# Low weight halves made in block 0, kept in DRAM, and loaded by the later blocks, in a float32 hybrid encoder layer on one core

## Chip, cores and metric

One Trainium2 chip, one core of it. The metric is device microseconds of one execution of the whole kernel, lower is better. Kernel before: median 4028.33 us of three runs (4001.9 to 4049.22).

## What is computed

One layer of a streaming encoder, on 2048 prompt frames and 32 sample frames, width 1024, all in float32 (`FF` is 2816):

```python
h = rmsnorm(x, g_pre_mix)
q, k, v, u, g = split_projection(h, w_in)          # u = u_a * sigmoid(u_b)
attn = prompt_attention(q, k, v, table, sink)      # 16 heads, window 128 + own chunk of 64
y = depthwise_conv(u_hist, w_dw) + b_dw            # width 31, 1024 channels
conv = silu(layernorm(y, ln_g, ln_b)) @ w_conv_out
m = g[:, :, 0] * attn + g[:, :, 1] * conv
x = x + rmsnorm(m @ w_out, g_post_mix)
h = rmsnorm(x, g_pre_ffn)
f = (silu(h @ w_ffn_gate) * (h @ w_ffn_up)) @ w_ffn_down
x = x + rmsnorm(f, g_post_ffn)
```

TensorE takes its fast four-byte type (fp32r), which keeps fewer bits than float32. So each operand `a` is split into `a_hi` (rounded to fp32r) and `a_lo = a - a_hi`, and each product is three: `hi*hi + hi*lo + lo*hi`.

## The kernel before

**Blocks and steps.** The tokens go in `NB` = 4 blocks of `T` = 512 columns; block 3 takes the 32 sample tokens too (544 columns, two groups of 272). Each block walks the same `NS` = 124 steps. One step is one 128x1024 float32 piece of weights (512 KB). The kinds, in order: 16 `glu_b`/`glu_a` (alternating), 8 `q`, 1 `k`, 1 `v`, 16 `gate`, 8 `conv`, 8 `out`, 44 `ffn_gate`/`ffn_up` (alternating), 22 `down`. The names `S_Q, S_K, S_A, S_C, S_W, S_F, S_D` are the first steps of q, k, gate, conv, out, ffn and down. `G(b, s) = b * NS + s` counts steps over the whole kernel; all 124 pieces are read anew in every block.

**Weights.** A piece passes three engines before TensorE (PE) may use it. SP loads it into one of `RAW` = 3 raw buffers (`load_weights`, L371), for the step three ahead, once `w_lo` of the piece that held the buffer is made. ScalarE (ACT) rounds it to `w_hi` (`split_hi`, L785); it waits for the raw piece and for `w_used`, that is for PE to have finished the step two before, since `w_hi` and `w_lo` have two buffers each. GpSimd (POOL) makes `w_lo = w_raw - w_hi` (`split_lo`, L465). PE waits for `w_lo` (`weights`), then does the step's matmuls, 24 of 512 columns as a rule (`feature_major`, L570; `token_major`, L606 to L608). ACT and POOL split the piece of step s+1 at the head of their work for step s.

**Beside the steps.** Every engine's order is written out by hand.
- VectorE (DVE) does the depthwise convolution, 248 tap instructions (`conv`, L1041 and L1045) a block, spread over steps 4 to 41 by `conv_ops`: 7 a step in glu, q, k, v, and 6 a step in the gate steps. Each is a SCALAR_TENSOR_TENSOR of two SBUF tensors, `y += u * dw`.
- Each of the 16 gate steps also carries one attention unit (4 heads x 128 queries): PE scores (L642 to L644), DVE `score_max` (L1108, writes `p`), ACT exponentials (`exps`, L875), DVE `denominator` (L1125, L1126), POOL `p * rl` (L510), PE transposes of `p` (L654), ACT `pt_hi` (L869), DVE `pt_lo` (L1120), PE product with the values (L671 to L673). `p` is one buffer: `score_max` of the next unit waits for the transposes of this one. PE's order in a gate step: scores(n), transposes(n-1), the step's 24 weight matmuls, values(n-1). DVE's order: `score_max(n)`, `pt_lo(n-1)`, 2 taps, `denominator(n)`, on odd n `qs_lo`, 4 taps.
- Step `S_C` waits for the LayerNorm of the convolution. After the last `out` step ACT, POOL and DVE do the norm after the mix and the one before the FFN, tile by tile (POOL L474, L476; DVE `scale_rows`, L1056), with the split of step `S_F + 1` between them; `first_ffn_steps` starts on the first tiles.
- At the end of a block the FFN's norm and residual run beside the first two steps of the next block (step 1 of block 3 waits for them on PE). In step 1 SP waits for that residual, and then stores the 2 MB block of `y_prompt` (`store_y`, L382).
- Further DMAs on SP's queue: `g_post` at `S_C`, 2 MB of x at `S_W`, 512 KB x tiles of the next block in `down`.

SP's loop body before, in the order of its issues, starts so:

```python
for b in range(NB):
    for s in range(NS):
        load_weights(G(b, s) + RAW)
        if s == 1 and b:
            store_y(b - 1)
```

## Time and profile before

| | |
|---|---|
| runs | 4028.33 us median, 4001.9 to 4049.22 |
| span of the profiled execution | 4055.0 us |
| PE matmul busy | 3463.3 us, 85% of the span |
| DVE / POOL / ACT busy | 2033.5 / 1602.4 / 1242.6 us (50 / 40 / 31%) |
| `w_lo` on POOL | 1337.3 us, 496 instructions |
| `w_hi` on ACT | 524.9 us, 496 instructions |
| DMA | 74 GB/s over the span, 289.22 MB read from HBM, 12.17 MB written |
| mean granted TensorE clock | 0.916 of full speed |

How to read it: busy is the time in which at least one instruction of the engine ran; matmuls are pipelined and their ends are modelled, so PE busy counts a little more than the work. A group's row reads: line, engine, operation, output <- inputs, shapes, count | busy us, mean ns of one | idle time of the engine just before, and what ended it. PEclk is the granted clock of TensorE as a share of full speed. Times in timelines are from the start of the span. The times of the runs are of other executions than the profiled one.

### The profile page before, as it was taken

Reading aid. Unit: us, or ns where it says so; the run is one execution under the profiler, and the core shown is the slowest. Engines: PE = TensorE matmul, PEld = TensorE weight load, DVE = VectorE, ACT = ScalarE, POOL = GpSimd, SP = SyncE. Lnnn points to the kernel's source line nnn. Section 1 sums busy time; section 2 is a strip of 40 time slices with the busy share of each in tenths; the row PEclk is TensorE's granted clock in tenths of the full one; section 3 lists DMA queues with packets and bytes.
Section 4 is the critical chain, followed back from the end, with each engine's and each line's share of the span. In section 5 each row is a group of like instructions: output and inputs, shape, how many; then the busy total and the mean of one; then the engine's idle time right before and its main releaser. Section 6 shows DMA issues by size and latency. Waiting matters only on the chain.

```text
span 4055.0 us, 42574 instructions
## 1 busy us (share of the span) xinstructions
PE 3463.3 (85%) x17022; PEld 2870.9 (71%) x17022; DVE 2033.5 (50%) x2660; ACT 1242.6 (31%) x1986; POOL 1602.4 (40%) x778
## 2 busy tenths in 40 slices
PE   2378877999997878999979878999978878969997
PEld 2256656887776656887757656887878866869986
DVE  1296963004599962005696962005495963230033
ACT  1013452224323442224213452224212433122222
POOL 1154433444444433444453433444454422233432
PEclk8689988999999988999989988999988976679999
DMA  1212112223321112233311112223211110212221
GB/s 58 82 63 68 47 47 84 99 95 108 114 83 47 47 64 82 94 98 106 113 60 55 47 58 85 96 94 110 100 58 59 48 32 31 71 47 89 86 81 60
DMA packets 88165, 300.92 MB, mean 74 GB/s; under 512 B 10338, under 2 KB 17586, under 8 KB 87330
## 3 DMA queue, kind: packets, MB, share of 16 engines
q1 hardware_dynamic: 87968, 298.21, 22.0%
q8 instruction: 135, 2.21, 0.2%
q14 instruction: 62, 0.50, 0.0%
HBM read 289.22 MB, written 12.17 MB: 74 GB/s over the span
## 4 chain that ended last, share of the span: by engine, by line
PE 56%; DVE 18%; issue 13%; POOL 9%; ACT 3%; DMA 1%; SPq 0%; POOLq 0%; DVEq 0%; ACTq 0%
PE PS L570 35%; DVE y L1045 12%; POOL w_lo L465 6%; PE PS L606 5%; PE PS L608 5%; PE PS L607 5%; POOL p L510 3%; PE PS L684 1%; PE PS L690 1%; DVE PS L1086 1%; PE PS L587 1%; DVE p L1108 1%; DVE x L1091 1%; DVE xs L1056 1%; DVE pt_lo L1120 1%
## 5 line engine op out<-in xcount | busy, mean ns | idle before, releaser
L465 POOL TENSOR_TENSOR w_lo<-w_raw,w_hi 128x1024 fp32r<-128x1024 f32 x496 | 1337.3, 2697 | 1791.8 <-ACT w_hi L785 1790.7
L570 PE MATMUL PS<-h_hi,w_hi 128*128 128x512 f32 (+1 forms) x3352 | 1088.9, 358 | 241.8 <-POOL w_lo L465 185.6
L785 ACT ACTIVATE w_hi<-w_raw 128x1024 fp32r<-128x1024 f32 x496 | 524.9, 1058 | 2077.9 <-PE PS L570 1502.0
L570 PE MATMUL PS<-h_hi,w_lo 128*128 128x512 f32 (+1 forms) x3352 | 1084.1, 357 | 0.0
L570 PE MATMUL PS<-h_lo,w_hi 128*128 128x512 f32 (+1 forms) x3352 | 1075.2, 354 | 0.0
L1045 DVE SCALAR_TENSOR_TENSOR y<-u,dw,y 128x512 f32<-128x512 f32 (+1 forms) x960 | 1011.5, 1118 | 0.0
L570 PEld LDWEIGHTS PS<-h_hi,w_hi 128*128 128x128 f32 x3352 | 601.2, 192 | 334.0 <-POOL w_lo L465 184.2
L570 PEld LDWEIGHTS PS<-h_lo,w_hi 128*128 128x128 f32 x3352 | 601.2, 192 | 90.2
L570 PEld LDWEIGHTS PS<-h_hi,w_lo 128*128 128x128 f32 x3352 | 599.0, 192 | 84.3
L1290 DVE TENSOR_TENSOR f<-PS,tmp 128x512 f32<-128x512 f32 (+1 forms) x88 | 61.6, 700 | 892.6 <-PE PS L570 868.6
L510 POOL TENSOR_TENSOR p<-p,small 128x1024 f32<-128x1024 f32 x68 | 157.2, 2312 | 464.8 <-DVE small L1126 464.8
L1296 DVE TENSOR_TENSOR f_lo<-f,f_hi 128x1024 fp32r<-128x1024 f32 (+1 forms) x88 | 208.9, 2374 | 249.5 <-ACT f_hi L999 249.5
L606 PE MATMUL PS<-w_hi,f_hi 128*128 128x512 f32 x748 | 296.7, 397 | 12.2 <-DVE f_lo L1296 8.4
L608 PE MATMUL PS<-w_hi,f_lo 128*128 128x512 f32 x748 | 295.1, 394 | 0.0
L607 PE MATMUL PS<-w_lo,f_hi 128*128 128x512 f32 x748 | 294.2, 393 | 0.0
L875 ACT ACTIVATE p<-p,small 128x256 f32<-128x256 f32 x272 | 135.1, 498 | 280.5 <-DVE small L1115 280.5
L606 PEld LDWEIGHTS PS<-w_hi,f_hi 128*128 128x128 f32 x748 | 140.5, 188 | 48.1 <-DVE f_lo L1296 10.8
L570 PE MATMUL PS<-act_hi,w_hi 128*128 128x512 f32 x320 | 131.8, 452 | 46.4 <-DVE act_lo L1260 46.4
L608 PEld LDWEIGHTS PS<-w_hi,f_lo 128*128 128x128 f32 x748 | 140.5, 188 | 33.0
L607 PEld LDWEIGHTS PS<-w_lo,f_hi 128*128 128x128 f32 x748 | 140.5, 188 | 32.5
L552 PE MATMUL PS<-ident_sb,xs 128*128 128x128 f32 x272 | 54.5, 368 | 108.5 <-DVE xs L1056 108.5
L1108 DVE CUSTOM_DVE_ANT_0 p<-PS,bias,sink_sb 128x256 f32<-128x256 f32 x272 | 114.9, 475 | 37.5 <-PE PS L654 27.8
(166 smaller groups left out, 3800.3 us busy)
## 6 DMA issues: line engine op xcount, KB each, us to landing
w_raw<-in_w_stream SPq DMA_DIRECT2D x496, 512.0 KB, 3.3
xs<-in_x_prompt SPq DMA_DIRECT2D x16, 512.0 KB, 3.7
x<-in_x_prompt SPq DMA_DIRECT2D x4, 2048.0 KB, 8.5
out_y_prompt<-x SPq DMA_DIRECT2D x4, 2048.0 KB, 7.3
gp<-in_g_post SPq DMA_DIRECT2D x4, 1024.0 KB, 4.8
toep_dram<-toep_dram SPq DMA_DIRECT2D x1, 3048.0 KB
bias<-toep_dram SPq DMA_DIRECT2D x1, 2048.0 KB, 8.6
bias<-toep_dram SPq DMA_DIRECT2D x2, 1024.0 KB, 5.8
```

Source lines behind the costliest of these rows:

```text
L465: nc.gpsimd.tensor_tensor(w_lo[:, g % 2, :], w_raw[:, g % RAW, :], w_hi[:, g % 2, :].bitcast(F32), ALU.subtract).then_inc(w_lo_ok, 1)
L510: nc.gpsimd.tensor_tensor(p[:], p[:], rl.unsqueeze(2).broadcast_to([P, 4, 2 * P]), ALU.mult).then_inc(p_ok, 1)
L570: last = nc.tensor.matmul(PS[:, k0 + off, 0:n], w, x[:, k, c0:c0 + n], start=first and k == 0, stop=stop and k == KT - 1)
L606: nc.tensor.matmul(out, hi, wk[0], start=first, stop=False)
L607: nc.tensor.matmul(out, hi, wk[1], start=False, stop=False)
L608: last = nc.tensor.matmul(out, lo, wk[0], start=False, stop=last_k)
L785: A(w_hi[:, g % 2, :], w_raw[:, g % RAW, :], ACT.Copy).then_inc(w_hi_ok, 1)
L875: A(p[:, h, :], p[:, h, :], ACT.Exp, bias=nmx[:, h:h + 1], accum_out=lsum[:, h:h + 1])
L1045: ins = STT(out, src, dw[:, ct, k:k + 1], out, ALU.mult, ALU.add)
L1108: nc.vector.tensor_tensor_reduce(out=p[:, h, :], in0=PS[:, 2 + h // 2, (h % 2) * 2 * P:(h % 2 + 1) * 2 * P], in1=bias[:, head, :], scale=1 ...
L1290: TT(over(b, f[:, j, 0:c]), z(b, r), over(b, tmp[:, j % 2, 0:c]), ALU.mult).then_inc(z_dve, 1)
L1296: TT(f_lo[:, dd % 2, :, 0:c], f[:, 2 * kp:2 * kp + 2, 0:c], f_hi[:, dd % 2, :, 0:c].bitcast(F32), ALU.subtract).then_inc(flo_ok, 1)
```

## The change

In block 0 nothing changes in how weights are split, but SP also stores each `w_lo` piece to a DRAM tensor (`keep_lo`). In blocks 1 to 3 SP loads two 512 KB pieces a step into the three raw buffers, the raw piece and its low half from DRAM (`load_halves`), for the step two ahead; ACT copies both with rounding, one into `w_hi` and one into `w_lo`; POOL makes no `w_lo`; PE waits for the count `w_got` of ACT's copies. A raw buffer is free again when ACT has copied the half that stood in it. `j = half(g, lo)` numbers the loads: one a step in block 0, two a step after.

```diff
+        w_lo_dram = nc.dram_tensor("w_lo_dram", [NS, P, D], F32, kind="Internal").ap()
...
+        def half(g, lo):
+
+            return g if g < NS else NS + 2 * (g - NS) + lo
...
-            def load_weights(g):
+            def load_half(j, src):
+
+                if j >= NS + RAW:
+                    sp.wait_ge(w_got, j - RAW - NS + 1)
+                elif j >= RAW:
+                    sp.wait_ge(w_lo_ok, j - RAW + 1)
+                sp.dma_start(w_raw[:, j % RAW, :], src).then_inc(raw_in[j % RAW], 16)
+
+            def load_halves(g):
                 if g >= NB * NS:
                     return
-                if g >= RAW:
-                    sp.wait_ge(w_lo_ok, g - RAW + 1)
-                sp.dma_start(w_raw[:, g % RAW, :], w_stream[g % NS]).then_inc(raw_in[g % RAW], 16)
+                s = g % NS
+                load_half(half(g, 0), w_stream[s])
+                sp.wait_ge(lo_out[s % 2], 16 * (s // 2 + 1))
+                load_half(half(g, 1), w_lo_dram[s])
+
+            def keep_lo(g):
+
+                sp.wait_ge(w_lo_ok, g + 1)
+                sp.dma_start(w_lo_dram[g], lo_of(g).bitcast(F32)).then_inc(lo_out[g % 2], 16)
...
             for b in range(NB):
                 for s in range(NS):
-                    load_weights(G(b, s) + RAW)
+                    if b == 0:
+                        keep_lo(s)
+                        if s + RAW < NS:
+                            load_half(s + RAW, w_stream[s + RAW])
+                    if G(b, s) + 2 >= NS:
+                        load_halves(G(b, s) + 2)
                     if s == 1 and b:
                         store_y(b - 1)
...
             def split_lo(g):
-                if g is None:
+                if g is None or g >= NS:
                     return
                 pool.wait_ge(w_hi_ok, g + 1)
                 if g >= 2:
                     pool.wait_ge(w_used, g - 1)
+                    pool.wait_ge(lo_out[g % 2], 16 * (g // 2))
...
             def weights(g):
-                pe.wait_ge(w_lo_ok, g + 1)
+                if g < NS:
+                    pe.wait_ge(w_lo_ok, g + 1)
+                else:
+                    pe.wait_ge(w_got, 2 * (g - NS) + 2)
...
-                act.wait_ge(raw_in[g % RAW], 16 * (g // RAW + 1))
+                j = half(g, 0)
+                act.wait_ge(raw_in[j % RAW], 16 * (j // RAW + 1))
                 if g >= 2:
                     act.wait_ge(w_used, g - 1)
-                A(w_hi[:, g % 2, :], w_raw[:, g % RAW, :], ACT.Copy).then_inc(w_hi_ok, 1)
+                if g < NS:
+                    A(hi_of(g), w_raw[:, j % RAW, :], ACT.Copy).then_inc(w_hi_ok, 1)
+                    return
+                A(hi_of(g), w_raw[:, j % RAW, :], ACT.Copy).then_inc(w_got, 1)
+                j = half(g, 1)
+                act.wait_ge(raw_in[j % RAW], 16 * (j // RAW + 1))
+                act.wait_ge(lo_out[g % 2], 16 * (NS // 2))
+                A(lo_of(g), w_raw[:, j % RAW, :], ACT.Copy).then_inc(w_got, 1)
```

`hi_of(g)` and `lo_of(g)` are the buffers `w_hi[:, g % 2, :]` and `w_lo[:, g % 2, :]` as before; PE's matmuls and their order are the same.

**POOL, the gate steps of block 1.** Before, `w_lo` pieces and the attention units' products `p * rl` take turns (x16 each; three of them shown):

```order
111 L510 TENSOR_TENSOR p<-p,small 128x1024 [waits rl_ok]
112 L465 TENSOR_TENSOR w_lo<-w_raw,w_hi 128x1024 [waits w_used,w_hi_ok]
113 L510 TENSOR_TENSOR p<-p,small 128x1024 [waits rl_ok]
114 L465 TENSOR_TENSOR w_lo<-w_raw,w_hi 128x1024 [waits w_used,w_hi_ok]
115 L510 TENSOR_TENSOR p<-p,small 128x1024 [waits rl_ok]
```

After, on POOL at the same place, with what stands just before (the norm of block 0's end) and behind (the gates of `S_C`):

```order
203 L520 TENSOR_TENSOR prs<-prs,neghalf 128x1 [waits pool_chain]
204 L542 TENSOR_TENSOR p<-p,small 128x1024 [waits rl_ok] x16
205 L549 TENSOR_TENSOR gates<-gates,q 128x512 [waits o_out,sig_ok]
```

From block 1 on the only large products on POOL are those of attention and of the gates; between the end of block 0 and the gate steps of block 1 it has none.

**ACT, two gate steps of block 1.** Before (`gates` is the copy of a gate result out of PSUM, `q` the copy of an attention result, `p` the exponentials):

```order
448 L875 ACTIVATE p,small<-p,small 128x256 [waits mx_ok]
449 L875 ACTIVATE p,small<-p,small 128x256 x3
450 L876 ACTIVATE small<-small 128x4
451 L852 ACTIVATE qs_hi<-q 128x512 [waits z_act,qk_done]
452 L785 ACTIVATE w_hi<-w_raw 128x1024 [waits w_used,raw_in1]
453 L925 ACTIVATE gates<-PS 128x512 [waits w_used]
454 L869 ACTIVATE pt_hi<-PS 128x1024 [waits pv_done,pt_done]
```

and after:

```order
481 L918 ACTIVATE p,small<-p,small 128x256 [waits mx_ok]
482 L918 ACTIVATE p,small<-p,small 128x256 x3
483 L919 ACTIVATE small<-small 128x4
484 L895 ACTIVATE qs_hi<-q 128x512 [waits z_act,qk_done]
485 L824 ACTIVATE w_hi<-w_raw 128x1024 [waits w_used,raw_in1]
486 L828 ACTIVATE w_lo<-w_raw 128x1024 [waits lo_out1,raw_in2]
487 L968 ACTIVATE gates<-PS 128x512 [waits w_used]
488 L912 ACTIVATE pt_hi<-PS 128x1024 [waits pv_done,pt_done]
```

One more ACTIVATE of 128x1024, which waits for a second load, stands ahead of `gates` and `pt_hi`.

**SP, where block 1 begins.** Before, the store of y stands among single loads:

```order
33 L371 DMA w_raw<-in_w_stream 128x1024 [waits w_lo_ok] x18
34 L382 DMA out_y_prompt<-x_60 128x4x1024 [waits pn_ok]
35 L371 DMA w_raw<-in_w_stream 128x1024 [waits w_lo_ok] x41
```

After, it stands between pairs; row 277 is the low half of step 3 of block 1, rows 279 and 280 are the pair of step 4:

```order
271 L397 DMA w_lo_dram<-w_lo 128x1024 [waits w_lo_ok]
272 L384 DMA w_raw<-in_w_stream 128x1024 [waits w_lo_ok]
273 L384 DMA w_raw<-w_lo_dram 128x1024 [waits w_got,lo_out1]
274 L384 DMA w_raw<-in_w_stream 128x1024 [waits w_got]
275 L384 DMA w_raw<-w_lo_dram 128x1024 [waits w_got,lo_out0]
276 L384 DMA w_raw<-in_w_stream 128x1024 [waits w_got]
277 L384 DMA w_raw<-w_lo_dram 128x1024 [waits w_got,lo_out1]
278 L408 DMA out_y_prompt<-x_60 128x4x1024 [waits pn_ok]
279 L384 DMA w_raw<-in_w_stream 128x1024 [waits w_got]
280 L384 DMA w_raw<-w_lo_dram 128x1024 [waits w_got,lo_out0]
```

Before, the load issued just ahead of the store was that of step 4; after, it is that of step 3.

## Rows read from the trace of the kernel before

**Rows 1.** The page: the span, and the chain that ended last, by line.
```profile
span 4055.0 us, 42574 instructions
...
PE PS L570 35%; DVE y L1045 12%; POOL w_lo L465 6%; PE PS L606 5%; PE PS L608 5%; PE PS L607 5%; POOL p L510 3%; PE PS L684 1%; PE PS L690 1%; DVE PS L1086 1%; PE PS L587 1%; DVE p L1108 1%; DVE x L1091 1%; DVE xs L1056 1%; DVE pt_lo L1120 1%
```
**Rows 2.** Stretches: us; PE, PEld, DVE, ACT, POOL busy; PEclk, DMA share, GB/s.
```profile
1071.00:1174.00 103.00, 93.46 (x386) 74.63 (x385) 91.20 (x103) 25.04 (x34) 47.55 (x28) 0.95 0.29 100
1174.00:1236.00 62.00, 60.18 (x311) 50.68 (x309) 62.00 (x63) 15.07 (x20) 27.09 (x10) 1.00 0.28 91
1236.00:1427.00 191.00, 156.72 (x780) 123.75 (x780) 185.13 (x320) 80.29 (x201) 82.93 (x31) 0.96 0.14 45
...
1966.00:2067.00 101.00, 91.78 (x386) 73.40 (x385) 89.59 (x101) 25.06 (x34) 50.02 (x28) 0.97 0.30 107
2067.00:2159.00 92.00, 66.78 (x308) 55.00 (x307) 61.63 (x80) 14.55 (x19) 48.13 (x10) 0.83 0.18 57
2159.00:2340.00 181.00, 156.87 (x784) 124.08 (x783) 172.09 (x304) 80.39 (x199) 79.38 (x31) 0.98 0.14 47
...
2882.00:3000.00 118.00, 101.59 (x769) 100.57 (x768) 93.19 (x115) 25.00 (x33) 51.92 (x28) 0.93 0.27 93
3000.00:3102.00 102.00, 74.33 (x551) 73.72 (x550) 67.11 (x83) 15.20 (x19) 51.37 (x10) 0.85 0.15 52
3102.00:3290.00 188.00, 165.46 (x1167) 151.25 (x1166) 178.31 (x309) 81.52 (x202) 79.28 (x31) 0.97 0.14 44
...
1620.00:1780.00 160.00, 160.00 (x697) 130.68 (x696) 9.71 (x15) 38.04 (x44) 69.83 (x29) 1.00 0.29 96
```
**Rows 3.** The two splits, each line by itself: count, ns min/median/max.
```profile
L465 POOL TENSOR_TENSOR w_lo<-w_raw,w_hi x496: 2339/2411/21333, 43.0 to 4019.4; 128x1024 fp32r<-128x1024 f32 x166
...
L785 ACT ACTIVATE w_hi<-w_raw x496: 1038/1061/1067, 41.8 to 4018.3; 128x1024 fp32r<-128x1024 f32 x166
```
**Rows 4.** Timeline of DVE over one gate step of block 1: start, us.
```profile
1275.09 0.47 DVE L1108 CUSTOM_DVE_ANT_0 p<-PS,bias,sink_sb 128x256 f32<-128x256 f32 x1
...
1277.10 1.22 DVE L1120 TENSOR_TENSOR pt_lo<-PS,pt_hi 128x1024 fp32r<-128x1024 f32 x1
...
1279.84 6.48 DVE L1045 SCALAR_TENSOR_TENSOR y<-u,dw,y 128x512 f32<-128x512 f32 x4
1286.25 0.47 DVE L1108 CUSTOM_DVE_ANT_0 p<-PS,bias,sink_sb 128x256 f32<-128x256 f32 x1
```
**Rows 5.** Timeline of POOL over the same gate step.
```profile
1280.00 2.31 POOL L510 TENSOR_TENSOR p<-p,small 128x1024 f32<-128x1024 f32 x1 [6.71 <-DVE small L1126]
1282.28 2.83 POOL L465 TENSOR_TENSOR w_lo<-w_raw,w_hi 128x1024 fp32r<-128x1024 f32 x1
```
**Rows 6.** Timelines of POOL and of DVE in the q steps of block 2.
```profile
2085.79 22.23 POOL L465 TENSOR_TENSOR w_lo<-w_raw,w_hi 128x1024 fp32r<-128x1024 f32 x2 [10.14 <-ACT w_hi L785]
...
2083.35 19.96 DVE L1045 SCALAR_TENSOR_TENSOR y<-u,dw,y 128x512 f32<-128x512 f32 x30
```
**Rows 7.** Timeline of ACT in the FFN steps of block 1.
```profile
1642.04 1.06 ACT L785 ACTIVATE w_hi<-w_raw 128x1024 fp32r<-128x1024 f32 x1 [4.46 <-PE PS L570]
...
1647.56 1.06 ACT L785 ACTIVATE w_hi<-w_raw 128x1024 fp32r<-128x1024 f32 x1 [3.98 <-PE PS L570]
```
**Rows 8.** DMA issues: count, KB each, median us from issue to landing.
```profile
w_raw<-in_w_stream SPq DMA_DIRECT2D x496, 512.0 KB, 3.3
...
x<-in_x_prompt SPq DMA_DIRECT2D x4, 2048.0 KB, 8.5
```
**Rows 9.** The beginning of block 1: timelines of SP and of ACT.
```profile
1086.19 0.39 SPq L382 DMA_DIRECT2D out_y_prompt<-x  x1
...
1096.22 1.06 ACT L785 ACTIVATE w_hi<-w_raw 128x1024 fp32r<-128x1024 f32 x1 [6.22 <-DMA w_raw<-in_w_stream]
```
**Rows 10.** Timeline of DVE in the norms before the FFN, block 1: two tiles' scaling.
```profile
1579.42 2.82 DVE L1056 TENSOR_SCALAR xs<-x,rstd 128x1024 f32<-128x1024 f32 x1 [0.72 <-POOL rstd L476]
...
1586.52 0.75 DVE L1056 TENSOR_SCALAR xs<-x,rstd 128x1024 f32<-128x1024 f32 x1 [0.73 <-POOL rstd L476]
```

More of the change, by code:

```diff
@@ L171, in build @@
         w_hi_ok, w_lo_ok = sem("w_hi_ok"), sem("w_lo_ok")
-        w_used = sem("w_used")
+        w_used, w_got = sem("w_used"), sem("w_got")
+        lo_out = [sem("lo_out0"), sem("lo_out1")]
         z_act, z_dve = sem("z_act"), sem("z_dve")
@@ L233, in result_out, with hi_of, lo_of @@
                 eng.wait_ge(z_dve, by_dve(b, s))
+        def hi_of(g):
+            return w_hi[:, g % 2, :]
+        def lo_of(g):
+            return w_lo[:, g % 2, :]
+        def half(g, lo):
+            return g if g < NS else NS + 2 * (g - NS) + lo
         def norm_tile(b, tt, second):
@@ L393, in _ @@
             for g in range(RAW):
-                load_weights(g)
+                load_half(g, w_stream[g])
             for tt in range(1, 4):
@@ L565, in feature_major @@
                         pe.wait_ge(alo_ok, b * KT + k + 1)
-                    hi, lo = (w[:, g % 2, k * P:(k + 1) * P] for w in (w_hi, w_lo))
-                    for w, x, first, stop in ((hi, x_hi, True, False), (hi, x_lo, False, False),
-                                              (lo, x_hi, False, True)):
+                    hi, lo = (t[:, k * P:(k + 1) * P] for t in (hi_of(g), lo_of(g)))
+                    for wt, x, first, stop in ((hi, x_hi, True, False), (hi, x_lo, False, False),
+                                               (lo, x_hi, False, True)):
                         for c0, n, off in parts:
-                            last = nc.tensor.matmul(PS[:, k0 + off, 0:n], w, x[:, k, c0:c0 + n],
+                            last = nc.tensor.matmul(PS[:, k0 + off, 0:n], wt, x[:, k, c0:c0 + n],
                                                     start=first and k == 0, stop=stop and k == KT - 1)
@@ L583, in first_ffn_steps @@
                         for k in range(KT):
-                            hi, lo = (w[:, g % 2, k * P:(k + 1) * P] for w in (w_hi, w_lo))
-                            for w, x, first, stop in ((hi, h_hi, True, False), (hi, h_lo, False, False),
-                                                      (lo, h_hi, False, True)):
-                                last = nc.tensor.matmul(out, w, x[:, k, c0:c0 + n],
+                            hi, lo = (t[:, k * P:(k + 1) * P] for t in (hi_of(g), lo_of(g)))
+                            for wt, x, first, stop in ((hi, h_hi, True, False), (hi, h_lo, False, False),
+                                                       (lo, h_hi, False, True)):
+                                last = nc.tensor.matmul(out, wt, x[:, k, c0:c0 + n],
                                                         start=first and k == 0, stop=stop and k == KT - 1)
@@ L600, in token_major @@
                         hi, lo = x_hi[:, kts[kk], t0:t0 + P], x_lo[:, kts[kk], t0:t0 + P]
-                        wk = [w[:, g % 2, kk * T:(kk + 1) * T] for w in (w_hi, w_lo)]
+                        wk = [t[:, kk * T:(kk + 1) * T] for t in (hi_of(g), lo_of(g))]
                         first, last_k = i == 0 and kk == 0, i == n_half - 1 and kk == 1
@@ L619, in values_of @@
                         hi, lo = h_hi[:, k, t0:t0 + P], h_lo[:, k, t0:t0 + P]
-                        wk = [w[:, g % 2, k * P:(k + 1) * P] for w in (w_hi, w_lo)]
+                        wk = [t[:, k * P:(k + 1) * P] for t in (hi_of(g), lo_of(g))]
                         nc.tensor.matmul(out, hi, wk[0], start=k == 0, stop=False)
```

## The prediction, made before the changed kernel was run

> **What bounds the kernel now.** I read the page first: its span and the chain that ended last. Then the busy times by stretch, since the kernel goes through stages with different limits, and last the timelines at the places where PE is not busy. The chain [rows 1] runs mostly over PE's weight matmuls, but DVE's taps have 12% of it, `w_lo` on POOL 6% and `p * rl` 3%. So something beside PE holds it for a fifth of the time, and the reader is to find where.
>
> The stretches [rows 2] answer that. They are, for blocks 1, 2 and 3, the glu steps, the q, k, v steps and the gate steps, and as the last row a piece of the FFN. In the FFN PE is busy for 160.00 of 160 us at full granted clock; `w_hi` copies follow each other there every 1647.56 - 1642.04 = 5.52 us [rows 7], which is PE's own pace for a step of 512 columns. Nothing can be won there. In glu PE has 9.5, 9.2 and 16.4 us without work, in q, k, v 1.8, 25.2 and 27.7 us, in the gate steps 34.3, 24.1 and 22.5 us. In two q, k, v stretches the granted clock is also down, at 0.83 and 0.85.
>
> The timelines show why. On DVE one gate step lasts from `score_max` at 1275.09 to the next at 1286.25, 11.16 us, and the four taps at its end take 6.48 us [rows 4]. Thirty taps with nothing beside them that gets through take 19.96 us, 0.665 each [rows 6], so four should take 2.7. The missing 3.8 us lie exactly beside the two POOL products [rows 5]: `p * rl` (2.31) and `w_lo` (2.83). DVE and POOL do not run side by side here; each stops the other. In the q steps it is turned round: two `w_lo` need 22.23 us while DVE runs its thirty taps, and one reaches 21.3 us against a median of 2.4 [rows 3, 6]. PE then waits for `w_lo`.
> By the Trainium skill, page "SBUF — State Buffer", section "SBUF: two separate sides", a DVE operation with two SBUF inputs and a POOL operation exclude each other for the whole instruction, and whichever starts first has the port. The first half agrees with these rows; by the second half POOL would wait for one tap of 0.7 us and not for thirty, so there the trace decides.
>
> **The change part by part.**
>
> *POOL loses 372 of 496 `w_lo`.*
> (a) q, k, v. No `w_lo` can starve there. Block 1 shows the stage nearly without a stall, 62 us. Block 2 goes from 92 to 61, block 3 from 102 to 62 x 544/512 + 2 = 68, block 1 loses 1: 31 + 34 + 1 = 66 us.
> (b) Gate steps. DVE's step loses the part of the 3.8 us that `w_lo` causes. The first tap behind `p * rl` waits about 2.31 - 0.66 = 1.65; the rest, 2.2, is `w_lo`'s. 11.16 - 2.2 = 9.0, and steps with an odd unit have `qs_lo` more (128x512 like a tap, about 0.6): 9.3 on average. PE is busy for 156.72 / 16 = 9.8 us a step, an overcount, at a clock of 0.96; at full clock about 9.4. Both engines then have nearly the same load, so I take 9.6, with the first step longer: 155 us for the stage, 163 in block 3. That is 191 - 155, 181 - 155 and 188 - 163: 36 + 26 + 25 = 87 us. Bounds: if PE's busy time stays as it is (157, 157, 165), 81; if all of DVE's 16 x 2.2 came through in each block, 105. The bound from the other side is rival B.
> (c) glu. Fourteen taps (9.3 us) and one `u` (128x512 too, 0.7) now fit into two PE steps (11.04), where two `w_lo` with 2.2 each made 14.4. PE's floor is 16 x 5.52 = 88 us (94 to 97 in block 3). See (e) for what is given back.
> (d) Norms before the FFN. `w_lo` of step `S_F + 1` holds the scaling of tile 2 for 2.82 us instead of 0.75 [rows 10], on the way to PE's transposes; ACT's second copy puts 1.06 on the same chain ahead of it. Net 1.0 us a block, and about as much for the same in `down`: 6 us in all. Bounds: 0 to 12.
>
> *SP's queue.* (e) A pair is loaded for the step two ahead, not three. In step 1 SP waits for the residual and then puts the 2 MB of y into the queue. Before, the load behind it was that of step 5, and ACT got it at 1096.22, 10.0 us after the store [rows 9]. Now it is the pair of step 4. With the residual a microsecond earlier (POOL starts its norm without a `w_lo` in front) the first half arrives at about 1095.5, the second 1.3 to 1.7 later, and ACT is done near 1098; PE, which began the block at 1071, wants it at 1071 + 4 x 5.52 = 1093. That is 5 us lost in blocks 1 and 2; in block 3 PE itself waits for that residual in step 1 and the loads land meanwhile (12 us of wait remain). So glu goes 103 to 93, 101 to 93, 118 to 97 + 12 = 109: 27 us. Bounds: 17 to 36. Behind the store only SP's own later loads are queued, and ACT waits for those in order, so a late half also holds ACT's sigmoid; PE needs that only two steps later.
>
> *ACT gets 372 more copies* at 1.06 us [rows 3]. Steady state: `w_used` fires, both copies take 2.1 us, where copy and `w_lo` took 1.06 + 2.41 = 3.5 us before; PE needs the pair 5.52 us after. In a gate step ACT has 80.29 / 16 = 5.0 us of work [rows 2] and would have 6.1 of 9.6. The copies start when PE ends the weight matmuls; `pt_hi` stands behind them and `gates`: 3.2 us later, with an attention copy (two at 1.06, two of half the size); PE's values, scores and transposes, the rest of its step (9.4 - 5.5 = 3.9), come before `pt_hi` can start. Cover of half a microsecond, priced at nothing; if it fails, `pt_lo` and DVE's whole step come later (rival B).
>
> *DMA.* Two loads of 512 KB a step: 190 GB/s in the FFN, where one is 96 GB/s at a DMA share of 0.29 [rows 2], so 0.58. A load takes 3.3 us from issue to landing, 2 MB take 8.5 [rows 8]: 1.7 us more for each further 512 KB, 3.4 us a pair if loads overlap, against 5.52. The low half of step g+2 is issued when ACT has copied the high half of g+1 (1.1 us into PE's step g) and must be in ACT's hands some 8.7 us later; it takes 3.3 to 5. Hidden.
> By the Trainium skill, page "DMA: Bandwidth & Descriptors", section "Anatomy of one DMA — SWDGE (gpsimd) path", a DMA costs 2.0 us fixed and its bytes at 436 GB/s, 3.2 us here, and its "Rules for kernel authors" ask for 1 MiB or more per DMA; that speaks against many small loads. One load agrees with it. Two one after the other would be 6.4 us by the page, more than PE's step; that is rival A.
>
> *Block 0* stores 124 low halves. SP waits for `w_lo` there anyway before a load; the store goes ahead of that load. Three raw buffers cover it, except at the start where PE waits for the first late load: +2 us (0 to 10).
>
> **Sum.** -66 - 87 - 27 - 6 + 2 = -184 us. Against the profiled execution, 4055 - 184 = 3871. Its span is 27 us over the median of the runs; if that is only how the execution was taken, the median becomes 4028 - 184 = 3844. The stalls in q, k, v differ from block to block in one execution (2, 25, 28 us), so part of the 27 is likely one stall more, which the change removes in any case, and the true number lies nearer 3871 by that part. I take 3855.
>
> **The rivals.**
>
> *A, the other side: pairs do not overlap and a pair takes 2 x 3.3 = 6.6 us.* Three half buffers leave little ahead. Then 82 steps (conv, out, FFN, down) of blocks 1 and 2 take 1.08 us longer each, +177; the FFN of block 3 +24; glu +8 in place of -27; q, k, v -43 in place of -66; the gate steps keep -87: 79 us slower, 4107. It decides from about 6.3 us for a pair. Against it: the 8.5 us for 2 MB, which are four loads' bytes, and the low DMA share. 5%.
>
> *B, a new wait in the gate steps.* ACT's second copy makes `pt_hi` late, or the loop from transposes over scores, exponentials and `p * rl` holds at some 10.7 us. The gain there is half, 44: 3900. For it: half a microsecond of cover. Against it: ACT is busy 40% there. 13%.
>
> *C, nothing to be seen.* The stalls move: DVE, no longer stopped, is stopped by PE, and the starts of the blocks lose more (15 us each, twice) while the gate stage stays. Then only (a) less 30 is left: 3992 to 4020. 4%.
>
> *D, my forecast,* 3810 to 3890: 78%.
>
> **How the numbers follow.** One per cent, 40 us, is about what a measurement can tell from no change. D, B and most of C are beyond it on the fast side, A on the slow side: faster 0.92, same 0.03, slower 0.05. The range goes from 3805 (gate at its better bound, glu too, the lower base) to 3915 (rival B with the upper base), which leaves out A, C and little of D.
>
> **What the profile will show.** Right, if DVE taps in blocks 1 to 3 are long only beside `p * rl`; q, k, v are near 61 us and gate steps near 9.6; FFN steps stay at 5.52 us with the DMA share near 0.6; one PE stall of 5 us stands at step 4 of blocks 1 and 2. Wrong, if ACT's copies wait for DMA in FFN steps (A), or if gate steps stay over 10.5 us with PE waiting for `pt_lo` or `p` (B).

## The result, and the profile after

The changed kernel takes 3835.91 us (median of 4 runs, 3831.98 to 3857.77), the kernel before, run beside it, 4037.47 us (4 runs, 4001.9 to 4049.22): ratio 0.9505, 95% interval 0.9456 to 0.9555. The forecast was 3855, with 3805 to 3915 as its range. The profiled execution of after took 3835.48 us, with a span of 3833.6; the span of before's was 4055.0 [rows 1].

The page of after: span, busy times, and the chain that ended last.

```profile
span 3833.6 us, 43442 instructions
...
PE 3409.4 (89%) x17022; PEld 2850.4 (74%) x17022; DVE 1698.6 (44%) x2660; ACT 1596.7 (42%) x2358; POOL 586.3 (15%) x406
...
PE 74%; DVE 4%; ACT 3%; issue 1%; POOL 1%; DMA 0%; SPq 0%; DVEq 0%; ACTq 0%; POOLq 0%
```

DVE's taps had 12% of the chain and `w_lo` 6% [rows 1]; now all of DVE has 4% and all of POOL 1%. DVE is busy for 335 us less (1698.6 against 2033.5) with the same 2660 instructions: that is the time for which POOL had made its instructions longer. The line numbers of after are: `w_hi` L824 (L822 in block 0), `w_lo` by ACT L828, `w_lo` by POOL L497, taps L1088, weight matmuls L605. Groups of after: count, busy us and mean ns.

```profile
L824 ACT ACTIVATE w_hi<-w_raw 128x1024 fp32r<-128x1024 f32 x372 | 394.6, 1061 | 1177.9 <-PE PS L605 876.3
L1088 DVE SCALAR_TENSOR_TENSOR y<-u,dw,y 128x512 f32<-128x512 f32 (+1 forms) x960 | 837.9, 939 | 0.0
...
L497 POOL TENSOR_TENSOR w_lo<-w_raw,w_hi 128x1024 fp32r<-128x1024 f32 x124 | 322.1, 2598 | 487.3 <-ACT w_hi L822 369.6
L828 ACT ACTIVATE w_lo<-w_raw 128x1024 fp32r<-128x1024 f32 x372 | 387.6, 1042 | 4.0 <-DMA w_raw<-w_lo_dram 4.0
```

The second copy costs ACT 1.04 us, and in the whole kernel it waited 4.0 us for its DMA. Where the time went shows by stages, each measured from the last weight matmul of the stage ahead to its own last one (us; in a cell the time before, then after):

| | glu | q, k, v | gate | conv | out | FFN | down | block |
|---|---|---|---|---|---|---|---|---|
| block 0 | 254 / 260 | 93 / 61 | 184 / 192 | 92 / 90 | 46 / 46 | 273 / 273 | 130 / 130 | 1071 / 1051 |
| block 1 | 103 / 95 | 62 / 60 | 191 / 157 | 90 / 85 | 46 / 46 | 273 / 270 | 131 / 127 | 895 / 839 |
| block 2 | 101 / 95 | 93 / 60 | 181 / 157 | 91 / 85 | 46 / 46 | 273 / 270 | 132 / 128 | 916 / 840 |
| block 3 | 118 / 107 | 102 / 67 | 188 / 166 | 218 / 214 | 59 / 59 | 310 / 310 | 155 / 156 | 1150 / 1080 |

In blocks 1 to 3: glu -25, q, k, v -69, gate -80, conv -14, FFN -6, down -7, and block 0 -19: together 221, the difference of the spans. Stretches of after, to be laid beside [rows 2]: us; PE, PEld, DVE, ACT, POOL busy; PEclk, DMA share, GB/s.

```profile
1051.00:1147.00 96.00, 90.85 (x389) 73.79 (x388) 70.80 (x109) 40.47 (x50) 4.82 (x12) 0.98 0.57 198
1147.00:1207.00 60.00, 59.95 (x311) 50.77 (x309) 46.98 (x72) 24.13 (x29) 0.00 (x0) 1.00 0.50 176
1207.00:1364.00 157.00, 152.82 (x783) 125.92 (x784) 145.09 (x310) 98.91 (x223) 36.05 (x16) 0.97 0.32 108
...
1985.00:2046.00 61.00, 60.72 (x314) 51.42 (x312) 47.35 (x72) 24.64 (x30) 0.00 (x0) 1.00 0.51 176
...
2838.00:2906.00 68.00, 67.72 (x555) 67.58 (x554) 52.02 (x74) 24.85 (x30) 0.00 (x0) 1.00 0.46 157
...
1620.00:1780.00 160.00, 159.22 (x696) 129.80 (x695) 14.65 (x19) 69.34 (x77) 0.80 (x2) 1.00 0.56 196
```

In q, k, v PE has at most 0.3 us of idle time left; in block 1 it has 5 us in glu and 4 us in the gate stage, where it had 9.5 and 34.3. The FFN piece has a DMA share of 0.56, and PE is as busy as before; the 0.8 us without PE are the start of `down` at 1764.

### The profile page after: what moved, and what is told of

Read it like the earlier page. It is cut to its first block, busy times and chain, and to the rows that moved or that the text cites. A ratio compares the mean times of both kernels' runs of the same rounds, so it can differ in the third digit from the quotient of the medians.

```text
span 3833.6 us, 43442 instructions
## 1 busy us (share of the span) xinstructions
PE 3409.4 (89%) x17022; PEld 2850.4 (74%) x17022; DVE 1698.6 (44%) x2660; ACT 1596.7 (42%) x2358; POOL 586.3 (15%) x406
## 4 chain that ended last, share of the span: by engine, by line
PE 74%; DVE 4%; ACT 3%; issue 1%; POOL 1%; DMA 0%; SPq 0%; DVEq 0%; ACTq 0%; POOLq 0%
PE PS L605 47%; PE PS L641 6%; PE PS L643 6%; PE PS L642 6%; PE PS L689 1%; PE PS L677 1%; PE PS L622 1%; DVE PS L1129 1%; DVE x L1134 1%; PE PS L678 1%; PE PS L679 1%; PE PS L706 1%; PE PS L725 1%; PE PS L707 1%; PE PS L708 1%
## 5 line engine op out<-in xcount | busy, mean ns | idle before, releaser
L605 PE MATMUL PS<-h_hi,w_hi 128*128 128x512 f32 (+1 forms) x3352 | 1077.7, 355 | 147.5 <-POOL w_lo L497 118.9
L605 PE MATMUL PS<-h_hi,w_lo 128*128 128x512 f32 (+1 forms) x3352 | 1077.6, 355 | 0.0
L605 PE MATMUL PS<-h_lo,w_hi 128*128 128x512 f32 (+1 forms) x3352 | 1068.7, 352 | 0.0
L824 ACT ACTIVATE w_hi<-w_raw 128x1024 fp32r<-128x1024 f32 x372 | 394.6, 1061 | 1177.9 <-PE PS L605 876.3
L1088 DVE SCALAR_TENSOR_TENSOR y<-u,dw,y 128x512 f32<-128x512 f32 (+1 forms) x960 | 837.9, 939 | 0.0
L605 PEld LDWEIGHTS PS<-h_hi,w_hi 128*128 128x128 f32 x3352 | 594.7, 190 | 232.0 <-POOL w_lo L497 112.6
L605 PEld LDWEIGHTS PS<-h_lo,w_hi 128*128 128x128 f32 x3352 | 595.0, 190 | 89.9
L605 PEld LDWEIGHTS PS<-h_hi,w_lo 128*128 128x128 f32 x3352 | 593.8, 190 | 83.4
L497 POOL TENSOR_TENSOR w_lo<-w_raw,w_hi 128x1024 fp32r<-128x1024 f32 x124 | 322.1, 2598 | 487.3 <-ACT w_hi L822 369.6
L828 ACT ACTIVATE w_lo<-w_raw 128x1024 fp32r<-128x1024 f32 x372 | 387.6, 1042 | 4.0 <-DMA w_raw<-w_lo_dram 4.0
L822 ACT ACTIVATE w_hi<-w_raw 128x1024 fp32r<-128x1024 f32 x124 | 131.2, 1059 | 536.5 <-PE PS L605 331.1
L1339 DVE TENSOR_TENSOR f_lo<-f,f_hi 128x1024 fp32r<-128x1024 f32 (+1 forms) x88 | 134.1, 1524 | 331.5 <-ACT f_hi L1042 330.7
L605 PE MATMUL PS<-act_hi,w_hi 128*128 128x512 f32 x320 | 131.9, 452 | 46.3 <-DVE act_lo L1303 46.3
```

Source lines behind the costliest of these rows:

```text
L497: nc.gpsimd.tensor_tensor(w_lo[:, g % 2, :], w_raw[:, g % RAW, :], w_hi[:, g % 2, :].bitcast(F32), ALU.subtract).then_inc(w_lo_ok, 1)
L605: last = nc.tensor.matmul(PS[:, k0 + off, 0:n], wt, x[:, k, c0:c0 + n], start=first and k == 0, stop=stop and k == KT - 1)
L822: A(hi_of(g), w_raw[:, j % RAW, :], ACT.Copy).then_inc(w_hi_ok, 1)
L824: A(hi_of(g), w_raw[:, j % RAW, :], ACT.Copy).then_inc(w_got, 1)
L828: A(lo_of(g), w_raw[:, j % RAW, :], ACT.Copy).then_inc(w_got, 1)
L1088: ins = STT(out, src, dw[:, ct, k:k + 1], out, ALU.mult, ALU.add)
```

## Profile after: two places where PE still waits

The first gate step of a block. Timelines of ACT, DVE and PE in block 1 of after: start, us, what ended the idle time before.

```profile
1207.04 1.06 ACT L824 ACTIVATE w_hi<-w_raw 128x1024 fp32r<-128x1024 f32 x1 [8.18 <-PE PS L658]
1208.00 1.04 ACT L828 ACTIVATE w_lo<-w_raw 128x1024 fp32r<-128x1024 f32 x1
1208.95 0.58 ACT L966 ACTIVATE v_hi<-PS 128x512 fp32r<-128x512 f32 x1
1209.43 0.62 ACT L895 ACTIVATE qs_hi<-q 128x512 fp32r<-128x512 f32 x1
```
```profile
1210.24 0.68 DVE L1140 TENSOR_TENSOR qs_lo<-q,qs_hi 128x512 fp32r<-128x512 f32 x1
```
```profile
1211.18 0.55 PE L677 MATMUL PS<-k_hi,qs_hi 64*128 64x256 f32 x1 [4.23 <-DVE qs_lo L1140]
```

And that step as a stretch (columns as above):

```profile
1207.00:1222.00 15.00, 10.82 (x38) 8.82 (x39) 8.16 (x19) 6.57 (x15) 2.31 (x1) 0.66 0.20 71
```

PE waits for 4.23 us for `qs_lo`, which stands behind four ACT copies; the granted clock of the step is 0.66, a mixture of the 2.4 and the 1.2 GHz level. This step takes 14.8 us.

The fifth glu step of blocks 1 and 2 (step 4). SP, ACT and PE in block 1 of after:

```profile
1066.07 0.39 SPq L408 DMA_DIRECT2D out_y_prompt<-x  x1
```
```profile
1075.70 1.06 ACT L824 ACTIVATE w_hi<-w_raw 128x1024 fp32r<-128x1024 f32 x1 [11.12 <-DMA w_raw<-in_w_stream]
1076.98 1.06 ACT L828 ACTIVATE w_lo<-w_raw 128x1024 fp32r<-128x1024 f32 x1 [0.22 <-DMA w_raw<-w_lo_dram]
1077.94 0.58 ACT L954 ACTIVATE tmp<-PS 128x512 f32<-128x512 f32 x1
```
```profile
1078.66 0.76 PE L605 MATMUL PS<-h_hi,w_hi 128*128 128x512 f32 x1 [5.15 <-ACT tmp L954]
```

ACT has the raw half 9.6 us after the 2 MB store was issued and the low half 1.3 us later, and PE stands still for 5.15 us. The last half microsecond is the sigmoid `tmp` of step 2, which ACT does behind the two copies and which PE needs for step 4. The prediction had seen the sigmoid held up, and had taken it for needed only later.

## The experiments

Eleven kernels, in four groups; each group had runs of before beside it, and each ratio is against those. Stage and step times are of the one profiled execution of each kernel.

**Stores alone.** The changed kernel with every `w_lo` of block 0 stored and none loaded back: the two functions that say so are these, and POOL makes all 496 `w_lo` as before.

```diff
+        def kept(s):
+            return s < NS
+
+        def dram(g):
+            return False
```

> The kernel before, with one part of the change: block 0 also stores its 124 low halves in DRAM; nobody reads them, and POOL makes all 496 w_lo as before. Theory L (DVE and POOL exclude each other; w_lo on POOL in blocks 1 to 3 was the whole cost): the time of before, ratio 0.995 to 1.005, block 0 at about 1071 us give or take the stalls in its q steps. Rival S (the stores in block 0 shift or shorten block 0, which was 19 us shorter in the changed kernel's trace): ratio about 0.995, block 0 near 1051 us, its q, k, v steps near 61 us.

4041.75 us (10 runs), ratio 1.002 [0.9981, 1.0058]; block 0 takes 1072 us in its profile, 1071 before. The interval of the ratio, 16 us to either side, shows no cost of the stores, but the trace does: the first four steps of block 0 take 180.8 us in place of 175.9 (179.8 in the changed kernel). There POOL's third `w_lo` waits for the store of the first, which stands in SP's queue behind the DMAs of the start. The stores are not the cause of block 0's -19 us either.

**POOL rounds the loaded low half.** Loads as in the changed kernel, but for blocks 1 to 3 POOL makes `w_lo` out of the loaded low half and zeros, the same instruction as before with two inputs:

```diff
-                A(lo_of(g), w_raw[:, j % RAW, :], ACT.Copy).then_inc(w_got, 1)
+                    nc.gpsimd.tensor_tensor(halves[0], halves[1], zero[:].unsqueeze(1).broadcast_to([P, KT, P]),
+                                            ALU.subtract).then_inc(w_lo_ok, 1)
```

> The changed kernel, but POOL rounds the low half that came from DRAM into w_lo (a TENSOR_TENSOR of 128x1024 that subtracts a tile of zeros), where ACT copies it in the changed kernel. All loads are those of the changed kernel. Theory L: most of the gain is gone, since POOL again holds what DVE's taps need: ratio to before 0.985 to 1.01, gate steps at 11 to 12 us, stalls of 5 to 20 us in q steps. Rival P (the gain came from the low halves being ready in DRAM, from the shorter way from the raw piece to PE): ratio 0.95 to 0.96, gate steps at 9.6 us, because POOL's instruction no longer waits for ACT's.

4041.73 us (10 runs, 4019 to 4080), ratio 1.0039 [0.9992, 1.0086]: the whole gain is gone, with the DMAs of the changed kernel in place. Its gate stages are 191, 181 and 187 us, within 0.5 us of those of before. Timelines of POOL and DVE in one gate step of it:

```profile
1402.17 2.31 POOL L554 TENSOR_TENSOR p<-p,small 128x1024 f32<-128x1024 f32 x1 [6.71 <-DVE small L1172]
1404.44 2.84 POOL L501 TENSOR_TENSOR w_lo<-w_raw,zero 128x1024 fp32r<-128x1024 f32 x1
```
```profile
1402.01 6.48 DVE L1091 SCALAR_TENSOR_TENSOR y<-u,dw,y 128x512 f32<-128x512 f32 x4
```

They are the rows of before over again (2.31, 2.83 and 6.48 [rows 4, 5]). So the gain comes from POOL doing less, and not from the low halves being ready in DRAM.

**POOL copies the low half.** The same, with a copy that has one input:

```diff
+                    nc.gpsimd.tensor_copy(lo_of(g), w_raw[:, j % RAW, :]).then_inc(w_lo_ok, 1)
```

> As the kernel in which POOL rounds the low half, but with a TENSOR_COPY of 128x1024, which has one SBUF input. Theory L1 (any long POOL instruction that reads SBUF stops DVE's taps, whatever the number of its inputs): about the time of before, 0.99 to 1.01, gate steps 11 to 12 us. Rival L2 (only a POOL instruction with two SBUF inputs stops them): DVE's taps stay at 0.74 us beside it and the time is that of the changed kernel, about 0.95. In between, 0.96 to 0.98, if the copy is just shorter than the subtraction (2.4 us).

3914.84 us (3898 twice, 3931 and 3932), ratio 0.9691 [0.9637, 0.9745]: between the two. One gate step on POOL and DVE:

```profile
1250.65 2.31 POOL L552 TENSOR_TENSOR p<-p,small 128x1024 f32<-128x1024 f32 x1 [6.72 <-DVE small L1170]
1252.91 1.50 POOL L500 CAST w_lo<-w_raw 128x1024 fp32r<-128x1024 f32 x1
```
```profile
1250.49 5.13 DVE L1089 SCALAR_TENSOR_TENSOR y<-u,dw,y 128x512 f32<-128x512 f32 x4
```
```profile
L500 POOL CAST w_lo<-w_raw x372: 1036/1044/24450, 1047.0 to 3859.6; 128x1024 fp32r<-128x1024 f32 x186
```

With both products on POOL four taps take 6.48 us, with product and copy 5.13, with the product alone 4.37 (below). The last row (ns min, median, max) shows that the copy takes 1.04 us as a rule; beside the taps it took 1.50, and one lasted 24.45 us. A short operation starves as a long one does, and each q, k, v stage is 11 to 27 us longer than in the changed kernel. By the Trainium skill, page "SBUF — State Buffer", section "Who interferes with whom", a DVE instruction with two SBUF inputs contends with a GpSimd instruction that reads SBUF. The copy reads it, if with one input only, and the 5.13 us agree.

**Low halves from DRAM in some stages only.** Two kernels in which pairs are loaded for a part of the steps; the others are loaded and split as in block 0. `kept(s)` decides both what is stored and what is loaded:

```diff
+        def kept(s):
+            return s < S_C
```

> Low halves are kept and loaded for the 42 steps of glu, q, k, v and gate alone; for conv, out, FFN and down of every block POOL makes w_lo as before. Theory L: nearly the whole gain, since DVE has its taps only there; lost are the norms before the FFN and the transposes in down, 3 + 4 us in blocks 1 and 2 each: ratio 0.953 to 0.957, about 3850 us. Rival F (the 66 FFN and down steps with a pair of loads each were slowed by the loads, or sped by the missing w_lo): more than 15 us away from the changed kernel on either side.

3855.27 us (3853.3 to 3857.8), ratio 0.9555 [0.9501, 0.9608]. Blocks 1 and 2 take 850 and 852 us against 839 and 840. The pairs from `S_C` on are worth 10 to 12 us in each of blocks 1 and 2: the step `S_C` takes 50.0 and 50.2 us against 46.1, the rest is in the start of the FFN and in `down`; all other conv, out and FFN steps are as long with them as without (5.6 and 5.5 us). In block 3 it is the other way round: 1075 us without these pairs, 1080 with them.

```diff
+        def kept(s):
+            return s < S_A
```

> Low halves are kept and loaded for the 26 steps of glu, q, k and v alone; POOL makes w_lo for the gate steps and all later ones. Theory: the gains of the stages add up. With the time of the kernel that does it up to conv at 3855 and gate steps back at 11.2 to 11.8 us instead of 9.5, about 35, 24 and 22 us more in blocks 1 to 3: 3935 us, ratio about 0.975; the first gate step stays at 14.8, since DVE is not behind when it comes. Rival: the gate stage was only as long as it was because DVE came into it late; then it is near 155 us here too, and the time near 3855.

3932.97 us (3930 to 3953), ratio 0.9746 [0.9698, 0.9794]. Stretches of q, k, v and gate in block 1:

```profile
1148.00:1208.00 60.00, 59.91 (x311) 50.74 (x309) 48.04 (x72) 23.14 (x28) 2.39 (x1) 1.00 0.49 167
1208.00:1389.00 181.00, 156.94 (x780) 124.12 (x780) 172.12 (x304) 80.42 (x199) 78.85 (x31) 0.97 0.15 47
```

Glu and q, k, v are those of the changed kernel, and the gate stage is that of before in the blocks that had stalled in q, k, v (181). The gains add up, as the prediction had added them: 78 us lie between the medians of these two kernels, which differ in the gate steps alone; by their traces 72 of them are in the gate stages and most of the rest in the conv stages behind them.

**More loads.** The changed kernel, and in each FFN step one 512 KB copy from DRAM to DRAM more in block 1, two in block 2:

```diff
+                for _ in range(g // NS if S_F <= s < S_D and g < 3 * NS else 0):
+                    sp.dma_start(spare_dram[(g // NS - 1 + _) * 2 * FT + s - S_F], w_stream[s]).then_inc(third, 16)
```

> The changed kernel, with further DMAs of 512 KB on SP's queue behind each pair in the FFN steps, DRAM to DRAM and used by nobody: one a step in block 1 (three in all), two a step in block 2 (four in all). Theory M (DMAs on the queue overlap, and each further one costs the 1.3 to 1.7 us of its bytes): FFN steps of block 1 stay at 5.52 us (3 x 1.3 to 1.7 = 3.9 to 5.1), those of block 2 at 5.5 to 6.8, so 0 to 55 us longer in all. Rival A (they run one after the other at 3.3 us): 9.9 us a step in block 1, 13.2 in block 2, over 500 us longer.

3845.96 us (3833.7, 3834.5, 3857.4, 3858.8), ratio 0.953 [0.9474, 0.9585], with a span of 3832.7: no change (the median is 10 us higher because two of the four runs lie in the upper of two clusters, see below). FFN pieces of block 1 and of block 2:

```profile
1620.00:1740.00 120.00, 120.00 (x524) 98.00 (x523) 7.61 (x11) 49.48 (x55) 0.00 (x0) 1.00 0.80 283
2450.00:2590.00 140.00, 140.00 (x611) 114.33 (x610) 9.00 (x13) 60.31 (x64) 0.00 (x0) 1.00 0.99 380
```

Four transfers of 512 KB fit into a step of 5.52 us, 1.38 us each, and PE does not notice, though the DMA share is 0.99. The low halves have twice the room that they need, but no more than that: with four transfers a step ACT begins to wait for raw halves, 48 us in all between 2345 and 2600 and up to 4.0 us at a time, which PE's steps still cover.

**The two places.** In one kernel the residual's 2 MB are stored in four parts, each behind its own tile:

```diff
+                for tt in range(4):
+                    sp.wait_ge(pn_ok, post_tile(b, tt, 1) + 1)
+                    sp.dma_start(y_prompt[b * T + tt * P:b * T + (tt + 1) * P, :],
+                                 x1[:, tt, :]).then_inc(y_out, 16)
```

> The changed kernel, with the 2 MB store of y in step 1 cut into four stores of 512 KB, each issued when its own 128 rows are done. Theory Q (the pair of step 4 stands behind 2 MB on the queue, and PE stalls there for 5 us and then runs some us at half clock): step 4 of blocks 1 and 2 falls from 12.4 and 11.7 us to about 6, 12 us less in all, ratio to before 0.947. Rival: the pair is late because SP itself waits for the last residual, then nothing changes, 0.950.

3821.75 us (3816.6 to 3841.9), ratio 0.9488 [0.942, 0.9556]. PE at step 4 of block 1:

```profile
1076.84 0.47 PE L606 MATMUL PS<-h_hi,w_hi 128*128 128x512 f32 x1 [1.56 <-ACT tmp L955]
```

The stall of 5.15 us is 1.56 (in block 2 it was 4.39 and is 0.59), and with less of it the clock hardly falls behind it: step 4 takes 7.3 and 6.4 us in the two blocks where it took 12.4 and 11.7, 10 us together for 7.4 us less of stall. The medians are 14 us apart. Another 5 us come from the end of the kernel, where the last block of y is now stored in four parts too: from PE's last weight matmul to the end of the span it is 17.9 us in e4, e8 and e10, and 22.9 in the changed kernel.

On top of it, the weight split of step `S_A` put behind the copies of v and `qs_hi`:

```diff
-                    split_hi(split_step(b, s))
+                    if s != S_A:
+                        split_hi(split_step(b, s))
...
+                                split_hi(split_step(b, s))
```

> The changed kernel with the store of y in four parts and, in step S_A (the first gate step), ACT's copies of the next pair behind the copy of v and the first qs_hi instead of ahead of them. Theory: PE waits 4.2 us at that step for scores, half of it for those two copies (2.1 us), and then runs its 24 matmuls at half clock (7.8 us in place of 5.8); the step falls from 14 to 15 us to 10 to 12.5, so 6 to 15 us less than the kernel with four stores (3822): 3807 to 3816. Rival: the wait is DVE's (v_lo, qs_lo) and nothing changes.

3816.71 us (five of 3812 to 3821, one of 3835.9), ratio 0.9453 [0.9415, 0.9491]. PE at the first gate step of block 2:

```profile
2059.11 0.55 PE L678 MATMUL PS<-k_hi,qs_hi 64*128 64x256 f32 x1 [2.28 <-DVE qs_lo L1143]
```

The wait is 2.28 us in place of 4.23 (the same in blocks 1 and 2 of either kernel). The first gate steps take 12.7, 12.0 and 14.9 us in place of e4's 14.1, 14.7 and 16.5: 5.7 us in blocks 1 to 3, and 5 by the medians. That is just short of the 6 to 15 that were expected, since half of the wait is that of `v` and q themselves.

**The clusters.** The runs of one kernel are not spread evenly: the changed kernel had 3832, 3835, 3836 and 3858, the e7 kernel 3834 twice, 3857 and 3859. The 52 runs of before in all groups lie at 4000 to 4007 (7 runs), 4019 (1), 4027 to 4033 (15), 4043 to 4055 (24) and 4069 to 4074 (5). The profile of e8's kernel fell on its one run of 3835.9, and shows what such a run has. POOL in block 0:

```profile
277.68 22.58 POOL L498 TENSOR_TENSOR w_lo<-w_raw,w_hi 128x1024 fp32r<-128x1024 f32 x2 [9.79 <-ACT w_hi L823]
```

Block 0 there has q, k, v of 93 us and a gate stage of 180; in the profile of the changed kernel these are 61 and 192. That is 20 us net, one cluster. Nine profiled kernels have the stores and no wait against this in block 0: seven of them have 61 us there, and two, e1 and e8, have 93. To test it, the kernel before got a wait on DVE ahead of its taps in the q steps, with no work added:

```diff
                     if s < S_A:
+                        if S_Q < s <= S_K:
+                            dve.wait_ge(w_lo_ok, G(b, s) + 1)
                         done = conv(b, done, conv_ops(s))
```

> The kernel before, with one wait more: in q steps 2 to 8 and the k step VectorE starts its seven taps only when w_lo of that step is made. No work is added or left out. Theory S (the steps of some 22 us between the runs of one kernel are blocks in which GpSimd's w_lo starves behind thirty taps): no w_lo can wait for more than seven taps (4.7 us), so no block has the stall; q, k, v stages 62 to 64 us in blocks 0 to 2 and 68 to 70 in block 3, gate stages at the length that belongs to it (about 191 us in blocks 0 to 2), the longest w_lo under 8 us; all runs within 10 us of each other and at the lowest cluster of before, 3995 to 4008 us, span of the profiled execution about 3998. Rival T (the steps come from elsewhere, such as the granted clock or the DMA queues, and the starved w_lo only goes with them): the runs still spread over 4001 to 4050 us, median about 4030, though q, k, v stages are short. It also prices how much of the changed kernel's gain three waits could have had: by theory S some 30 us of 200.

4006.89 us (3994 to 4016, 4 runs), ratio 0.9897 [0.9846, 0.9949]: 41 us less than before beside it. So a wait without any other change is worth a fifth of the whole change's 202. POOL in block 2:

```profile
2064.89 9.45 POOL L465 TENSOR_TENSOR w_lo<-w_raw,w_hi 128x1024 fp32r<-128x1024 f32 x2 [10.18 <-ACT w_hi L785]
```

The stretches of q, k, v in blocks 2 and 3:

```profile
2046.00:2116.00 70.00, 62.21 (x311) 51.99 (x309) 67.76 (x75) 14.63 (x19) 30.68 (x10) 0.95 0.22 75
2960.00:3056.00 96.00, 82.45 (x549) 81.32 (x548) 70.29 (x82) 14.90 (x19) 41.87 (x10) 0.83 0.16 55
```

Theory S holds in its direction and roughly in its size, but its stage times were too good and its runs spread over 22 us where 10 were expected. The wait begins at the second q step, and the taps ahead of it still starve one `w_lo` (two took 9.45 us in place of 22.2). In block 3 the stage is 96 us and not 70: PE waits 13.5 us in five places there, and then runs the v step at the 1.2 GHz level (granted clock 0.50 from 3042 to 3056), so that the step takes 26.9 us in place of 13.3 with a wait of only 2.3 ahead of it. Why `w_lo` is late four times in that block is open. The same wait in block 0 alone, where all else that could starve is gone, is the cleaner test. First in the kernel of e8, and below it in the changed kernel itself (e11):

```diff
+                        if b == 0 and S_Q < s <= S_K:
+                            dve.wait_ge(w_lo_ok, s + 1)
```

> The kernel of e8 (changed kernel, y stored in four parts, weight split late at the first gate step) with the same wait before VectorE's taps, in block 0 only, where GpSimd still makes w_lo. Theory S: the runs lie in one cluster, none at 3835 or above, median 3808 to 3818 us (the lower cluster of e8 is 3812 to 3821); q, k, v of block 0 62 to 64 us. Rival T: one run in four or more is some 20 us longer, as in e8 and in the changed kernel.

3811.78 us (3809.4 to 3814.0, 4 runs), ratio 0.9419 [0.9365, 0.9473]; the best kernel of the study.

> The changed kernel with one edit: in block 0, q steps 2 to 8 and the k step, VectorE starts its seven taps only when w_lo of that step is made. e10 had four runs in one cluster, but with one run in four of the upper cluster that happens by chance in a third of the cases; so here more runs. Theory S: every run in 3825 to 3840 us, none at 3850 or above, median about 3834. Rival T: about one run in four at 3855 to 3860 us, as in the changed kernel and in e7 (three of eight).

3833.98 us (3831.3 to 3838.5, 6 runs), ratio 0.949 [0.9452, 0.9527]. Ten runs of the two, all in the lower cluster; without the wait 5 of 18 runs of the changed kernel, e4, e7 and e8 were in the upper one. At that rate ten in a row have a chance of (13/18)^10 = 4%, and of 9% if one allows that the rate itself comes from 18 runs. That an upper run has the stall in block 0 is shown by one profile, that of e8; that the wait removes it is likely and not certain. For the kernel before, in which each of the four blocks could have such a stall, theory S is inferred from the sizes and from e9.

## Why the prediction was right, step by step

**(a) q, k, v: -66 forecast, -69 measured.** Right, with its mechanism: no POOL product and no PE stall is left there.

**(b) Gate steps: -87 forecast, -80 measured.** The step itself was right: DVE in a gate step of block 1 of after,

```profile
1344.00 0.69 DVE L1140 TENSOR_TENSOR qs_lo<-q,qs_hi 128x512 fp32r<-128x512 f32 x1
1344.61 4.37 DVE L1088 SCALAR_TENSOR_TENSOR y<-u,dw,y 128x512 f32<-128x512 f32 x4
1348.90 0.47 DVE L1151 CUSTOM_DVE_ANT_0 p<-PS,bias,sink_sb 128x256 f32<-128x256 f32 x1
```

has four taps of 4.37 us beside `p * rl`, 2.11 less than the 6.48 of before [rows 4] where 2.2 was forecast, and the fifteen later steps take 9.5 us on average in blocks 1 and 2 and 10.0 in block 3. The term that was mis-sized is the first step, given 11 us (the stage's 155 less fifteen steps of 9.6); it takes 14.8, 15.3 and 16.5 (before 23.6, 14.4 and 16.5, so in blocks 2 and 3 it gained nothing). I had priced ACT's second copy at nothing for want of a place where it is not covered; it has one there, and it brings the lower clock level with it. The e8 kernel moved both copies away and got 5.7 us of this back.

**(c) and (e) glu: -27 forecast, -25 measured.** The stall at step 4 was forecast as 5 us and is 5.15 in block 1 and 4.39 in block 2. What the forecast left out is the clock behind it: the step takes 12.4 us in block 1, which is 1.7 more than 5.52 and 5.15. The taps did fit into two PE steps: fourteen take 9.36 us, every 11.04.

**(d) Norms and `down`: -6 forecast, -13 measured.** Both halves exist, and each was twice its forecast, though all of it is in blocks 1 and 2. In the norm of block 1, by the timelines, PE waits for the third tile for 4.94 us, against 6.54 before, and a wait of 0.88 for `w_lo` is gone. In `down` three waits of 1.39, 0.58 and 0.57 us for `f_lo`, which DVE had to compute beside `w_lo`, are gone: 2.5 us, while the steps with them are 3.5 us shorter.

**Left out: the start of the conv stage, -14.** PE in block 1 before, and in block 1 of after:

```profile
1431.37 1.09 PE L654 MATMUL PS<-ident_sb,p 128*128 128x128 f32 x8 [2.35 <-POOL p L510]
...
1438.54 9.13 PE L684 MATMUL PS<-y,ones 128*128 128x512 f32 x16 [0.78 <-ACT q L862]
```
```profile
1365.52 1.09 PE L689 MATMUL PS<-ident_sb,p 128*128 128x128 f32 x8 [0.53 <-POOL p L542]
...
1372.69 7.11 PE L719 MATMUL PS<-y,ones 128*128 128x512 f32 x16 [0.78 <-ACT q L905]
```

PE waits for the last unit's `p` for 0.53 us in place of 2.35, and the sixteen matmuls of the mean take 7.11 us in place of 9.13. e3 tells which `w_lo` it was: there the gate steps have pairs and only step `S_C` has a `w_lo` on POOL, which stands ahead of that `p`; its rows are those of before:

```profile
1367.97 1.09 PE L714 MATMUL PS<-ident_sb,p 128*128 128x128 f32 x8 [2.34 <-POOL p L567]
...
1375.14 9.20 PE L744 MATMUL PS<-y,ones 128*128 128x512 f32 x16 [0.78 <-ACT q L930]
```

One POOL instruction at the wrong place costs 4 us there, in blocks 1 and 2. The 1.8 us of the wait are the same in every trace in which POOL subtracts there. The other 2 only go with it as a rule, since the mean's matmuls took 7.1 us in nine of twelve such blocks of kernels with pairs, and in two of twelve without. In block 3 the wait for the last `p` is 0.53 us before and after, and e3's step `S_C` takes 103.7 us, the changed kernel's 106.6: the 4 us there are not explained. I had asked for `w_lo` beside taps, and not for `w_lo` ahead of `p` where the weight steps end and cover nothing more.

**Block 0: +2 forecast, -19 measured, and not by the change.** e1 has the stores and a block 0 of 1072 us. The wait at the start that was forecast is there, and costs 4 us where 2 was given. Against it stands the cluster of the last section, 24 us: q, k, v less 32 and the gate stage plus 8. The profiled execution of before had the stall in block 0, that of after did not.

**The sum.** From the profiled execution 3871 was forecast and 3835 came: 21 of the 36 us are block 0, nearly all of it chance, 14 the conv start, 7 (d), 3 (a), and (b) gave back 7 and glu 2. I had argued that the extra 27 us of the profiled execution were likely one stall more that the change removes in any case. It had three (blocks 0, 2 and 3), and the change removes those of blocks 2 and 3; block 0's it cannot remove. The median as base gives 4028 - 184 = 3844, closer to the 3836 that came, but that is partly luck: 4028 was the median of three runs, and that of all 52 is 4046, from which 3862 would follow. Against before run beside it the change is worth 202 us by the medians, where 184 was forecast. The lower end of the range does not come out of its terms either: the lower base 3844 less 18 for the gate stage and 9 for glu is 3817, and 3805 was given.

**The rivals.** A is out: four transfers fit where it said that two do not (e7), and ACT waited 4.0 us in all for low halves, and in blocks 1 to 3 21 us for raw ones, all of it behind the store of y. By the Trainium skill, page "DMA: Bandwidth & Descriptors", section "Rules for kernel authors", bandwidth is highest with 1 MiB or more per DMA; here 512 KB each, back to back on one queue, moved 380 GB/s. B did not come as it was described: the gate steps behind the first take 9.5 and 10.0 us, under its 10.5, and what the second copy holds up is `qs_lo`, in the first gate step of a block. C is out: the gate stage gave 80 us.
